# Three model blocks on one core: new places for waiting work, and the S5 scan's result in the drive's PSUM bank

## The reference

```python
for layer in range(DEPTH):
    mod = (c_act @ ada_w[layer] + ada_b[layer])[:, None, :]
    shift_m, scale_m, gate_m, shift_f, scale_f, gate_f = jnp.split(mod, 6, axis=-1)
    h = _rmsnorm(x, norm_g[layer, 0]) * (1.0 + scale_m) + shift_m
    ...
    x = x + gate_m * mix
    h = _rmsnorm(x, norm_g[layer, 1]) * (1.0 + scale_f) + shift_f
    x = x + gate_f * (jnp.square(jax.nn.relu(h @ w_fc1[layer])) @ w_fc2[layer])
...
# S5, for each of 64 groups of 16 channels and both directions
    bu_re = jnp.einsum('sgc,gpc->sgp', us, bb_re[direction])
    ...
    _, _, h_re, h_im = lax.associative_scan(
        _s5_combine, (a_re, a_im, bu_re, bu_im), reverse=(direction == 1), axis=0)
    y = y + (jnp.einsum('sgp,gcp->sgc', h_re, cr[direction])
             - jnp.einsum('sgp,gcp->sgc', h_im, ci[direction]))
z = jax.nn.gelu(y + d_skip * u)
return (z @ w_glu_a) * jax.nn.sigmoid(z @ w_glu_b)
```

## Time and profile before

| | |
|---|---|
| median of 3 runs | 1359.84 us (1357.15 to 1360.2) |
| profiled execution | 1358.06 us, its span 1356.3 us |
| mean granted TensorE clock | 0.951 |
| PE busy | 1238.4 us (91%) |
| DVE, ACT, POOL busy | 844.7, 534.5, 404.5 us |
| chain that ended last | PE 61%, POOL 13%, DVE 10%, ACT 5%, DMA 5%, issue 4% |

### The profile page before, as it was taken

One profiled execution on the slowest core, in us unless ns is written; L12 is line 12 of the kernel. 1 busy time (PEld: TensorE's weight loads), 2 busy tenths in 40 slices (PEclk: granted clock), 3 DMA queues, 4 the chain that ended last, 5 costly groups with the idle time before them and its releaser, 6 DMA issues.

```text
span 1356.3 us, 24531 instructions
## 1 busy us (share of the span) xinstructions
PE 1238.4 (91%) x10728; PEld 1150.8 (85%) x10728; DVE 844.7 (62%) x942; ACT 534.5 (39%) x679; POOL 404.5 (30%) x573
## 2 busy tenths in 40 slices
PE   5995998979898978889999999996999998999999
PEld 4884686979898958788999999796778998999998
DVE  6599764656577658845697443646765565566453
ACT  2130234434223243334555432455357734534341
POOL 7999625689879018700000000000000021000000
PEclk7897997989899998999999999998899999899999
DMA  9962656668879454246364555353133353355551
GB/s 351 392 237 94 232 199 243 218 218 317 306 286 325 177 209 154 88 145 248 119 221 167 183 184 185 124 187 124 63 124 125 125 186 128 125 184 186 172 202 63
DMA packets 120251, 258.20 MB, mean 190 GB/s; under 512 B 5056, under 2 KB 19024, under 8 KB 120016
## 3 DMA queue, kind: packets, MB, share of 16 engines
q1 hardware_dynamic: 91184, 196.18, 41.0%
q10 hardware_dynamic: 25504, 46.81, 9.6%
q0 software_dynamic: 3456, 13.63, 2.6%
...
## 4 chain that ended last, share of the span: by engine, by line
PE 61%; POOL 13%; DVE 10%; ACT 5%; DMA 5%; issue 4%; SPq 1%; ACTq 0%; DVEq 0%; POOLq 0%
PE bank L1840 61%; POOL tabw L710 4%; DVE big L1395 4%; POOL tabw L707 2%; POOL prep L715 2%; DMA ring<-in_w_in 1%; DVE ring_split L1335 1%; ACT ada_slot_split L869 1%; POOL big L777 1%; DMA ada_slot<-in_ada_w 1%; DVE rstd L1296 1%; SPq L581 1%; POOL tabw L715 1%; POOL big L770 1%; DMA ring<-in_w_glu_b 1%
## 5 line engine op out<-in xcount | busy, mean ns | idle before, releaser
L1840 PE MATMUL bank<-squares_split,ring_split 128*128 128x256 f32 x1056 | 301.8, 286 | 0.0
L1840 PEld LDWEIGHTS bank<-squares_split,ring_split 128*128 128x128 f32 x1056 | 206.0, 195 | 0.0
L783 POOL TENSOR_TENSOR y_cat<-y_cat,tmp 128x512 f32<-128x512 f32 x8 | 11.1, 1392 | 538.1 <-DVE tmp L1763 538.1
L1286 DVE SCALAR_TENSOR_TENSOR ada_acc<-ada_slot,cact,ada_acc 128x512 f32<-128x512 f32 x150 | 125.5, 837 | 5.0
L1840 PE MATMUL bank<-ada_slot_split,ring_split 128*128 128x256 f32 x432 | 122.2, 283 | 0.0
L1335 DVE TENSOR_TENSOR ring_split<-ring,ada_slot_split 128x2048 fp32r<-128x2048 f32 (+1 forms) x32 | 72.2, 2257 | 79.0 <-ACT ada_slot_split L869 79.0
L1840 PE MATMUL bank<-big_split,ring_split 128*128 128x256 f32 x352 | 100.7, 286 | 0.0
L1840 PE MATMUL bank<-h_in_split,ada_slot_split 128*128 128x256 f32 x272 | 79.0, 290 | 8.2 <-DVE y_cat_split L1746 3.8
L1840 PE MATMUL bank<-big_split,ada_slot_split 128*128 128x256 f32 x296 | 86.4, 292 | 0.0
L869 ACT ACTIVATE ada_slot_split<-ring 128x2048 fp32r<-128x2048 f32 (+1 forms) x32 | 60.2, 1884 | 64.1 <-PE bank L1840 32.5
L1840 PEld LDWEIGHTS bank<-ada_slot_split,ring_split 128*128 128x128 f32 x432 | 82.9, 192 | 0.0
...
## 6 DMA issues: line engine op xcount, KB each, us to landing
...
```

Of the source, the lines that this page charges most:

```text
L1286: stt(acc, w[:, i, :], cact[:, i:i + 1], acc, ALU.mult, ALU.add)\
L1840: return pe.matmul(*args, skip_group_check=True, **kw)
```

## The change

It has no new kind of work but one copy per S5 direction; nearly all else is order.

- **Mixer.** `convolve(1)` is cut at tap 11 of its two parts, with `add_taps(0)` between them (and `DVE_SLABS` goes from 6 to 7: DVE sums one slab more of each early modulation panel, PE four rows fewer). `residual(0)` has `ada_mod(8)` and `split_low(0)` after its first part, `ada_mod(9)` after its third, where both stood ahead of it.
- **S5 weights.** k = 1 moves ahead of `ms1`, k = 2 to 4 behind `f1.0.4`, `.10`, `.15` (k = 1 to 4 stood behind `.1`, `.5`, `.9`, `.13`), k = 5 to 7 one step later in `f2.0`.
- **Norms 1 and 3.** ACT writes the high part with the bias in one step, DVE's low part adds the bias itself.
- **S5 loop.** The scan writes into the drive's PSUM bank, q0 reads it there, ACT copies it to `gbuf` behind q0 (`scanned`), and POOL's multiplication waits for the copy (`s5c`). The drives have banks 0 to 5 of their own, z the upper halves of 6 and 7. `z_low` moves from the end of an odd iteration to its start, `dd` behind the first three drives, `mms` behind `z7`, the memory's norm behind GLU's second part, decay rows into `ada_acc`.
- **Second block.** `head_norm(0)` goes ahead of the GLA state update and `copy_predicated` ahead of `head_norm(1)`; a `split_low` goes between max and reciprocal of each softmax; `nr4` and `nr5` one u earlier; `split(BRANCH + 7)` behind the merged splits; `split(LAST + 2)` behind `residual(4)`.

```diff
-DVE_SLABS = 6
+DVE_SLABS = 7
...
-S5_AFTER = {1: 1, 5: 2, 9: 3, 13: 4}
+S5_AFTER = {4: 2, 10: 3, 15: 4}
-SIDE_S5 = {0: 5, 2: 6, 4: 7}
+SIDE_S5 = {1: 5, 3: 6, 5: 7}
...
-            "wo0.0", "ada7", "wo0.1", "wt0.0", "kl0", "wt0.1", "ada8", "wo0.2", "ada9", "wo0.3", "ms1"]
+            "wo0.0", "ada7", "wo0.1", "wt0.0", "kl0", "wt0.1", "ada8", "wo0.2", "ada9", "wo0.3", "wt1.0", "kl1", "wt1.1", "ms1"]
...
-        if u in (1, 2):
-            jobs.append(f"nr{3 + u}")
+        if u in (0, 1):
+            jobs.append(f"nr{4 + u}")
...
+            if name in S5_JOBS:
+                n = int(name[1:]) if name[0] != "d" else int(name[2:]) + 3
+                return bank[n % 6 if name[0] == "v" or name in ("dd0", "dd1", "dd2") else 7 if name == "dd3" else 6 + n % 2]
...
-                    pool.wait_ge(s("s5g"), m + 1)
+                    pool.wait_ge(s("s5c"), m + 1)
...
-                    act.activation(h[:, k, :], h[:, k, :], ACT.Identity, bias=mod[:, i:i + 1]).then_inc(s("h"), 1)
-                    if n in SPLIT_NORMS and k:
-                        input_high(n, k - 1)
...
+                    if n in SPLIT_NORMS:
+                        act.activation(input_parts(n)[0][:, k, :], h[:, k, :], ACT.Identity, bias=mod[:, i:i + 1]).then_inc(s("h_high"), 1)
...
+            def scanned(n):
+
+                act.wait_ge(s("s5q"), n + 1)
+                if n >= 2:
+                    act.wait_ge(s("s5r"), n - 1)
+                act.activation(gbuf[n % 2].rearrange("p q c t -> p (q c t)"), ps(f"v{n}")[:, :], ACT.Copy).then_inc(s("s5c"), 1)
...
+            for n in range(16):
+                scanned(n)
...
+                if n + 3 < 16:
+                    decay_row(n + 3)
+                if n >= 2 and n % 2 == 0:
+                    gelu(n // 2 - 1)
+                    if n // 2 + 2 < 8:
+                        negate(n // 2 + 2)
+                if n >= 3 and n % 2:
+                    high_part((n - 3) // 2)
...
-            for u in range(3):
+            for u in range(2):
                 split_high(LAST + u)
...
-            convolve(1, 0, DVE_TAPS)
+            convolve(1, 0, DVE_TAPS // 2)
             add_taps(0)
+            convolve(1, DVE_TAPS // 2, DVE_TAPS)
...
+            def between(p):
+                if p == 1:
+                    ada_mod(8)
+                    split_low(0)
+                elif p == 3:
+                    ada_mod(9)
+
+            residual(0, "wo0", 16, between)
...
             for n in range(17):
+                if n >= 5 and n % 2:
+                    z_low((n - 5) // 2)
...
-                    if m >= 2:
-                        dve.wait_ge(s("s5r"), m - 1)
...
+                    result = ps(f"v{m}")[:, :]
                     dve.tensor_tensor_scan(result, decays[m % 3], source, 0.0, ALU.mult, ALU.add).then_inc(s("s5g"), 1)
...
-                if n >= 5 and n % 2:
-                    z_low((n - 5) // 2)
...
+                if p == 1:
+                    memory_norm()
...
+            dve.wait_ge(s("gqs"), 2)
+            head_norm(0, gsc[:, 0:1], fq_n[:, 0:2, :])
             job_wait(dve, "cs1")
...
+            head_norm(1, gsc[:, 0:1], fq_n[:, 2:4, :])
+            split_low(PROJ + 10)
...
+                    split_low(GATES + u + 2)
                     dve.wait_ge(s("ue"), 2 * u + 2)
...
-                if n % 2 == 0:
+                if n % 2 == 0 and n < 10:
                     split_low(BRANCH + 2 + n // 2)
...
-            residual(4, "w2o", None, low6)
+            residual(4, "w2o", None, lows)
+            split_low(LAST + 2)
```

199 lines of the change are left out of this document (103 added, 96 removed).

## The result

The changed kernel takes **1347.29 us**, median of 7 runs (1344.72 to 1351.54), and the kernel before, run beside it, 1357.15 (7 runs, 1350.02 to 1360.2). The ratio is 0.9935 with a 95% interval of 0.9914 to 0.9955, so the kernel is faster, but by 9.9 us where 32 were forecast. It lies 1.3 us above the range that was given.

A forecast was written before the change was run, and what follows sets the result against it. PE work was taken to bind from 641.7 to 857.3 us, PE's waits elsewhere being winnable. Terms -8.4 - 12 + 3 - 9 - 5.5 = -31.9 took 1358.1 to 1326.2 profiled, given as 1328, range 1312 to 1346.

The forecast's parts named there:

- Mixer: Mixer and k = 1, up to ms1 and the norm behind it: term of -8.4 us.
- its own idle pieces: Mixer: DVE decides the stage's end and saves its idle pieces, 9 us up to the output projection.
- S5 weights: S5 weights in the feed-forward part: fewer waits for POOL; term of -12 us, between 0 and -15.
- everything ahead is earlier: Feed-forward part: later places give no more room, so k = 6 and 7 wait some 5 us each; 4 comes back.
- S5 loop and GLU: S5 loop with the GLU: pairs of directions go from 8.4 to 9.4 us; term of +3, between -7 and +7.
- holds up a panel's low part: GLU: the memory's norm, now lying there, delays a panel's low part, of which 1.5 us show.
- stands behind the copy of the scan just done (0.5) and four decay rows: S5 loop: ACT's queue makes `high_part` late for `z_low`, so DVE stands 2.2 us once per pair.
- gains from the free port: Rival, S5 loop: POOL's steps bind, a pair takes 7.4 us, 8 less; total about 1316; chance 0.12.
- The rival with the loop at 8.4: Rival, S5 loop: POOL is never late, pairs stay at 8.4, 6 us less than forecast, 1322; chance 0.13.
- Second block: Second block: GLA mask waits and `rstd` waits shrink; term of -9 us, between -3 and -13.
- 2.3 us for `nr4` "one u earlier": Second block: the rest of the `rstd` waits, 2.3 us, goes with `nr4` one u earlier.
- Merge and last residual: Merge and last residual: first waits caused by weight splits queued ahead go; term of -5.5, between -2 and -7.

The follow-up runs named there:

- experiment 4: Changed kernel with the S5 weights' k = 2 to 5 moved earlier in PE's order: 1346.87 us, ratio 0.9929.
- experiment 7: Changed kernel with the S5 weights' k = 2 to 5 and also k = 6 moved earlier in PE's order: 1337.39 us, ratio 0.9865.
- experiment 11: Changed kernel with Experiment 1, Experiment 3, experiment 7 and `shift(2)` first, but k = 1 back behind ms1 and k = 2 behind f1.0.3: 1318.26 us.
- Experiment 3: Changed kernel with the memory's norm ahead of the GLU's low parts instead of behind its second part: 1340.08 us, ratio 0.9882.
- experiment 2: Changed kernel with ACT's `high_part` ahead of the four decay rows in odd iterations: 1350.6 us, ratio 0.9951.
- Experiment 1: Changed kernel with `z_low` back at the end of an odd S5 iteration: 1335.95 us, ratio 0.9853.
- experiment 9: Changed kernel with Experiment 1, Experiment 3, experiment 7 and `shift(2)` first, plus drives made one direction further ahead: 1310.7 us, ratio 0.9673.
- experiment 5: Experiment 1 with the scan's result back in SBUF, without ACT's copies, six banks kept: 1336.11 us, ratio 0.9856.
- experiment 10: Changed kernel with Experiment 1, Experiment 3, experiment 7 and `shift(2)` first, but `nr4`, `nr5` back one u later: 1311.72 us, ratio 0.9678.
- experiment 15: Changed kernel with Experiment 1, Experiment 3, experiments 7, 9, 10 and `shift(2)` first, but weight splits back ahead of merged splits and `residual(4)`: 1317.4 us.

## Why the prediction was right or wrong

Nearly all the signs that the prediction named came: 4.9 us ahead of ms1, 4.1 and 4.0 ahead of k = 6 and 7, q0 at 0.69, a pair of 9.7, DVE idle before `z_low`, one wait of 4.7 at the mask. The time did not, because the largest misses lie where no sign had been named, in the loop's ends and behind the GLU.

**Mixer, -4.2 for -8.4.** The wait for k = 1 came as forecast (4.9 for 5), the one for `add_taps` at 2.9 instead of 1.2. The step that failed is the 9 us of "its own idle pieces", DVE's, "up to the output projection". DVE's timeline after:

```profile
149.40 2.47 DVE L1456 TENSOR_TENSOR tmp<-bank,memory_kv 128x512 f32<-128x512 f32 x4
...
154.02 0.71 DVE L1311 TENSOR_SCALAR ada_acc<-ada_slot,cact 128x512 f32<-128x512 f32 x1 [2.08 <-DMA ada_slot<-in_ada_w]
```

It reaches this rotary step at 149.40 in both kernels: up to there DVE had only 1.0 us of idle time in the kernel before, with the same panel sums in both. Its idle pieces lay behind that, the longest 4.34 us. Of the 14.2 us that PE is ahead at V, 8.6 are given back (5.2 in the wait for `ada_acc`), and DVE then waits 2.08 for a modulation panel's transfer. So 5.6 us are left at the start of the output projection where 9 were counted. From there to ms1 it went as forecast (+1.0 for +1.8), and the norm behind it got 0.45 longer instead of 1.2 shorter. The size is uncertain by some us: in the traces of the experiments with this mixer f1.0.0's first product starts between 223.8 and 230.4, and in the one of the kernel before at 229.8. No run tried the parts of the mixer apart.

**S5 weights, -8.5 for -12.** The two waits at k = 6 and 7 came, 4.1 and 4.0 for "some 5 us each", and k = 2's went. Failed: that the 2.6 us for `ada_acc` go (it is still 2.6 there), and the waits for `h_in_split` rose by 2.4, which weren't in the sum. The two waits were forecast, but for another reason (everything ahead is earlier): experiments 4 and 7 show that they come from places that are too late, where POOL stands until PE has read its tables. What moving k = 1 forward is worth stays open (experiment 11).

**S5 loop and GLU, +16.0 for +3: the term that failed.** The prediction's pieces, put where they act, against the differences in position:

| stretch | forecast | measured |
|---|---|---|
| ms2 to the first scan (`dd`, norm) | -1.5 | +0.5 |
| first to last scan (pairs +6, mean square gone -3.7) | +2.3 | +4.3 |
| last scan to the last outputs | nothing | +3.3 |
| to the first GLU product (mean square) | +2.5 | +2.4 |
| GLU to K (bank -2.1, memory's norm +1.5) | -0.6 | +5.5 |

- The memory's norm, the largest miss: it "holds up a panel's low part", "of which 1.5 us show". The GLU's own work did not lose (-1.9), but ms3 and K did, by 5.6 and 1.8. The step asked who waits on DVE, not who waits for the norm's result: SP's load, the loads behind it, ACT's split, ms3. Experiment 3 gives 7.8 us back by K.
- The pair: place right, reason wrong. That ACT's `high_part` is late because it "stands behind the copy of the scan just done (0.5) and four decay rows" is refuted by experiment 2. In its place stands the closed chain with `z_low` in it (experiments 1 and 9).
- The loop's end was put at nothing. `z_low` is in line there too: DVE stands 3.90 us for it at 563.80, PE then 4.28 for POOL's product, and its outputs at 570.08 take 3.68 us at a granted clock of 0.63. Experiment 1 has 7.1 us from the last scan to the last outputs, the changed kernel 9.3, the one before 6.0.
- Experiment 1 recovers 13 us by the end of the outputs, more than the 7.6 that were lost from the first scan to there, since the mean square's 3.7 us had left this stretch as well.
- The rival "gains from the free port" had the instructions right (q0 0.69, product 1.27) and the time wrong. The rival with the loop at 8.4 did not come either, but experiments 1 and 5 show it once `z_low` is back.

**Second block, -6.7 for -9.** The mask: 10.4 us of waits became 4.7, -7.3 for the forecast -6.5. Failed: 2.3 us for `nr4` "one u earlier". PE's waits for `rstd` do fall (6.3 to 4.7), and DVE's tabw step is late in their place, 4.3 us with a low clock behind; experiment 10 puts the cost at 6. The sum came near only because the stage's other edits, counted at nothing, gained about as much.

**Merge and last residual, -9.9 for -5.5.** The mechanism held; the waits shrank by 6.0 (7.4 to 1.4), near the forecast, and the clock behind them, which it did not count, gave the other 4 (experiment 15: 10.3 in all).
